# The first expert's rows of a mixture-of-experts layer picked out of SBUF by a 0/1 matrix on TensorE, with the DRAM gathers starting at the second expert and the weight requests in another order

## The reference, cut to what matters

```
h = LN1(alpha*x + m @ w_out)                    # 520 x 1024
g_prob = softmax(h @ w_group + b_group)         # one group of 4
e_logits = h @ w_router + b_router              # top 2 of the 4 experts inside it
for e in range(16):
    hid = silu(h @ w_gate[e]) * (h @ w_up[e])   # 1024 -> 512
    y += combine[:, e] * (hid @ w_down[e])      # 512 -> 1024
out = LN2(alpha*h + y)
```

## Time and profile before

| | |
|---|---|
| median of three runs | 939.65 us (938.61 to 940.93) |
| the profiled execution: its time | 937.05 us |
| its span | 935.2 us |
| mean granted TensorE clock | 0.963 |
| TensorE busy | 854.9 us, 91% of the span |
| VectorE busy | 545.4 us, 58% |
| ScalarE busy | 441.4 us, 47% |
| GpSimd busy | 173.1 us, 19% |
| DMA | 179.74 MB, 192 GB/s on average |

### The profile page before, as it was taken

How to read it: one execution, slowest core, us unless ns; L and a number is a source line. 1 busy time by engine, 2 the same in 40 slices (tenths; PEclk the granted TensorE clock), 3 DMA queues, 4 the chain that set the end, 5 groups by cost and what they waited for, 6 DMA issues and landing times.

```text
span 935.2 us, 13784 instructions
## 1 busy us (share of the span) xinstructions
PE 854.9 (91%) x5364; PEld 755.5 (81%) x5364; DVE 545.4 (58%) x613; ACT 441.4 (47%) x560; POOL 173.1 (19%) x151
## 2 busy tenths in 40 slices
PE   4999988889979899999999999489999999999990
PEld 4999976557759899999999877467888888888870
DVE  3112156665763333344222542769999999999976
ACT  4222232545553233233223211447788878778853
POOL 0085023321321000000000036141111111210103
PEclk9999999999999999999999999679999999999996
DMA  7422211810101212221221434799999999999953
GB/s 288 142 90 90 90 55 59 304 51 1 46 1 54 108 57 103 107 107 58 102 98 45 172 103 152 284 371 422 386 392 403 393 387 400 399 381 403 342 151 91
DMA packets 35835, 179.74 MB, mean 192 GB/s; under 512 B 3663, under 2 KB 11503, under 8 KB 19502
## 3 DMA queue, kind: packets, MB, share of 16 engines
q1 hardware_dynamic: 30182, 159.22, 44.1%
q0 software_dynamic: 5600, 19.99, 7.7%
q10 hardware_dynamic: 16, 0.03, 0.0%
HBM read 164.65 MB, written 16.89 MB: 194 GB/s over the span
## 4 chain that ended last, share of the span: by engine, by line
PE 84%; DVE 7%; ACT 4%; DMA 2%; issue 2%; POOL 0%; SPq 0%; DVEq 0%; ACTq 0%; POOLq 0%
PE ps L1116 8%; PE ps L1117 8%; PE ps L1118 8%; PE ps L1434 6%; PE ps L1435 6%; PE ps L1436 6%; PE ps L955 4%; PE ps L956 4%; PE ps L957 4%; PE ps L1461 3%; PE ps L1463 3%; PE ps L1462 3%; PE ps L1282 3%; ACT probs L627 2%; PE ps L1422 2%
## 5 line engine op out<-in xcount | busy, mean ns | idle before, releaser
L1920 DVE TENSOR_TENSOR elo<-eraw,ehi 128x2048 fp32r<-128x2048 f32 x96 | 218.0, 2290 | 26.2 <-ACT ehi L794 24.2
L794 ACT ACTIVATE ehi<-eraw 128x2048 fp32r<-128x2048 f32 x96 | 183.0, 1916 | 28.4 <-PE ps L1436 17.2
L1562 DVE TENSOR_TENSOR wlo<-raw,whi 128x2432 fp32r<-128x2432 f32 (+1 forms) x25 | 63.4, 2536 | 153.6 <-ACT whi L546 153.6
L1116 PE MATMUL ps<-xhi,whi 128*128 128x260 f32 x384 | 110.0, 286 | 3.5 <-DVE wlo L1736 3.5
L1117 PE MATMUL ps<-xhi,wlo 128*128 128x260 f32 x384 | 109.5, 285 | 0.0
L1118 PE MATMUL ps<-xlo,whi 128*128 128x260 f32 x384 | 109.4, 285 | 0.0
L1434 PE MATMUL ps<-ehi,xethi 128*128 128x512 f32 x256 | 103.3, 403 | 4.5 <-issue 3.2
L1435 PE MATMUL ps<-ehi,xetlo 128*128 128x512 f32 x256 | 101.2, 395 | 0.0
L1436 PE MATMUL ps<-elo,xethi 128*128 128x512 f32 x256 | 101.2, 395 | 0.0
L546 ACT ACTIVATE whi<-raw 128x2432 fp32r<-128x2432 f32 (+1 forms) x25 | 52.3, 2094 | 90.1 <-PE ps L1118 90.1
L1116 PEld LDWEIGHTS ps<-xhi,whi 128*128 128x128 f32 x384 | 73.6, 192 | 3.7 <-DVE wlo L1736 3.7
(11 more groups left out here) (365 smaller groups left out, 1887.0 us busy)
## 6 DMA issues: line engine op xcount, KB each, us to landing
eraw<-w_gate_in SPq DMA_DIRECT2D x32, 1024.0 KB, 18.1
eraw<-w_up_in SPq DMA_DIRECT2D x32, 1024.0 KB, 18.7
eraw<-w_down_in SPq DMA_DIRECT2D x32, 1024.0 KB, 20.3
raw<-wm_in SPq DMA_DIRECT2D x16, 1216.0 KB, 5.3
raw<-wz_in SPq DMA_DIRECT2D x8, 1024.0 KB, 5.3
raw<-wo_in SPq DMA_DIRECT2D x4, 1024.0 KB, 5.0
h_dram<-hall POOLq DMA_DIRECT2D x5, 416.0 KB, 3.5
f_dram<-hall POOLq DMA_DIRECT2D x5, 416.0 KB, 5.4
```

The costliest lines, as they stand in the source:

```text
L794: ac.activation(ehi[s % 3][:, :], eraw[s][:, :], ACT.Copy).then_inc(ehi_ok, 1)
L1116: pe.matmul(out, cols(whi[s], q), mh, start=k == 0, stop=False)
L1920: ve.tensor_tensor(elo[s % 3][:, :], eraw[s][:, :], ehi[s % 3][:, :].bitcast(F32), ALU.subtract)\
```

## The change

TensorE no longer waits for a gather of the first expert's rows. VectorE builds `hot0`, a 0/1 matrix of 5 x 104 tokens by 128 places for expert 0, between the two halves of the last tile's norm, and TensorE multiplies `hall` with it: 5 tiles x 8 feature groups = 40 true f32 products, whose result is the turned rows in the banks where the transposes used to put them. The slot list follows behind the picking. The weight list is made after wide product 0. Expert 1's rows are turned between the two halves of the second wide product. POOL's gathers run from expert 1 on, with the two `xe` buffers swapped. VectorE splits pieces 0 and 1 before it waits for the slot list, makes `xetlo` right after the slots, and splits piece 2 after the inputs of the weight list. SP sends pieces 3 and 8 before it waits for the rows in DRAM; pieces 4, 5, 9, 10 and on wait for the end of the picking instead of the first gather.

```diff
@@ buffers
-        gm, gd, gs = rt("gm", 2, [TR, TT]), rt("gd", 3, [TR, TT, 4]), rt("gs", 4, [TR, TT])
+        gm, gd, gs = rt("gm", 2, [TR, TT]), rt("gd", 29, [TR, TT, 4]), rt("gs", 30, [TR, TT])
+        place0, hot0 = rt("place0", 31, [TR, TT]), rt("hot0", 21, [TR, TT, CAP])
-        ltri = at("ltri", TAIL + 4096, [TR, NE, NE])
+        ltri = at("ltri", CON + 4 * C_MASK, [TR, NE, NE])
@@ SP
             sp.wait_ge(h_done, TT - 1)
             sp.wait_ge(h_last, 2)
+            expert_piece(3, 3, wu[0, 1], True)
+            expert_piece(8, 8, wd[0, 0], True)
             sp.wait_ge(h_sent, 16 * TT)
-            expert_piece(3, 3, wu[0, 1], True)
-            sp.wait_ge(xe_in[0], 16)
             sp.wait_ge(f_init, 16 * TT)
+            sp.wait_ge(xet_ps, 1)
             for n in range(2):
                 expert_piece(4 + n, 4 + n, wg[1, n], True)
-            for n in range(2):
-                expert_piece(8 + n, 8 + n, wd[0, n], True)
+            expert_piece(9, 9, wd[0, 1], True)
             expert_piece(10, 10, wg[2, 0], True)
@@ TensorE
+            pe.wait_ge(list_ok, 1)
+            pe.wait_ge(h_done, TT - 1)
+            for t in range(TT):
+                if t == TT - 1:
+                    pe.wait_ge(h_last, 2)
+                for k in range(KD):
+                    last = pe.matmul(ps[:, 4 + k // 4, (k % 4) * P:(k % 4) * P + P],
+                                     hall[:, t, :].rearrange("p (c k) -> p k c", k=KD)[:, k, :], hot0[:, t, :],
+                                     start=t == 0 and k % 4 == 0, stop=t == TT - 1, skip_group_check=True)
+            last.then_inc(xet_ps, 1)
+
             for n in range(2 * TT):
                 if n % TT == 0:
-                    pe.wait_ge(list_ok, n // TT + 1)
+                    pe.wait_ge(list_ok, n // TT + 2)
...
-            pe.wait_ge(list_ok, 3)
-            for n in range(2 * TT):
-                last = pe.matmul(ps[:, 7, P:P + NE], rowhot[...].bitcast(F32), chunkw[...], ...)
-            last.then_inc(slot_ps, 1)
+            def weight_list():
+                pe.wait_ge(list_ok, 4)
+                for n in range(2 * TT):
+                    last = pe.matmul(ps[:, 7, P:P + NE], rowhot[...].bitcast(F32), chunkw[...], ...)
+                last.then_inc(slot_ps, 1)
...
-            xet(0, 0, 16, True)
             pe.wait_ge(xet_hi, 1)
             pe.wait_ge(xet_lo, 1)
             wide(0, (0, 1), 0)
-            xet(1, 1, 16)
-            wide(2, (2, 0), 1)
+            weight_list()
+            wide(2, (2, 0), 1, between=lambda: xet(1, 0, 16))
@@ VectorE
             ve.tensor_tensor(x, x, lng[0:TR, :], ALU.mult).then_inc(h_last, 1)
+            ve.wait_ge(rank_ps, 1)
+            ve.wait_ge(rc_in, 16)
+            link(ve.scalar_tensor_tensor(place0[:, :], rank[:, :, 0], 1.0, both[:, :, 0], ALU.add, ALU.mult))
+            ve.scalar_tensor_tensor(hot0[:, :, :], row..., 1.0, place0..., ALU.add, ALU.is_equal).then_inc(list_ok, 1)
             ve.wait_ge(h_last, 1)
             ve.tensor_tensor(x, x, lnb[0:TR, :], ALU.add).then_inc(h_last, 1)
...
+            esplit(0, 0, True)
+            esplit(1, 1, True)
             ve.wait_ge(slot_ps, 1)
             found = ps[:, 6, P:P + NE]
             ve.tensor_scalar(slots[:, 0:NE], found, -1.0, float(T), ALU.min, ALU.add).then_inc(slot_ok, 1)
+            xet(0)
...
+            link(ve.tensor_copy(ltri[:, :, :], rcon...))
             ve.tensor_tensor(chunkw[:, :, :, :], picks..., wider(w12...), ALU.mult).then_inc(list_ok, 1)
-            esplit(0, 0, True)
+            esplit(2, 2, True)
             ve.wait_ge(slot_ps, 2)
             ve.tensor_copy(wslot[:, 0:NE], ps[:, 7, P:P + NE]).then_inc(wslot_ok, 1)
-            link(ve.tensor_copy(ltri[:, :, :], rcon...))
-            esplit(1, 1, True)
-            esplit(2, 2, True)
...
-            xet(0)
             esplit(3, 3)
@@ POOL
-                q = c % 2
-                if c >= 2:
-                    gp.wait_ge(xe_in[q], 16 * (c // 2))
+                q = 1 - c % 2
+                if c >= 3:
+                    gp.wait_ge(xe_in[q], 16 * ((c - 1) // 2))
                     gp.wait_ge(xet_ps, c - 1)
-                if c == 1:
+                if c == 2:
                     gp.wait_ge(xe_in[0], 16)
+                    gp.wait_ge(xet_ps, 1)
+                    gp.wait_ge(f_init, 16 * TT)
...
-            for c in range(NE):
+            for c in range(1, NE):
                 gather(c)
```

More of the change, by code:

```diff
@@ L1407, in _, with xet @@
             last.then_inc(slot_ps, 1)
-            pe.wait_ge(list_ok, 3)
-            for n in range(2 * TT):
-                last = pe.matmul(ps[:, 7, P:P + NE], rowhot[:, n // TT, n % TT, :].bitcast(F32),
-                                 chunkw[:, n // TT, n % TT, :], start=n == 0, stop=n == 2 * TT - 1)
-            last.then_inc(slot_ps, 1)
-            def xet(c, q, arrived, first=False):
+            def weight_list():
+                pe.wait_ge(list_ok, 4)
+                for n in range(2 * TT):
+                    last = pe.matmul(ps[:, 7, P:P + NE], rowhot[:, n // TT, n % TT, :].bitcast(F32),
+                                     chunkw[:, n // TT, n % TT, :], start=n == 0, stop=n == 2 * TT - 1)
+                last.then_inc(slot_ps, 1)
+            def xet(c, q, arrived):
                 pe.wait_ge(xe_in[q], arrived)
-                if not first:
-                    pe.wait_ge(xet_hi, c)
-                    pe.wait_ge(xet_lo, c)
+                pe.wait_ge(xet_hi, c)
+                pe.wait_ge(xet_lo, c)
                 for k in range(KD):
@@ L1424, in xet, with wide @@
                 last.then_inc(xet_ps, 1)
-            def wide(n, s, bank, first=False, free=None, hi=xethi, lo=xetlo):
+            def wide(n, s, bank, first=False, free=None, hi=xethi, lo=xetlo, between=None):
                 if free is not None:
@@ L1430, in wide @@
                 for j in range(2):
+                    if j and between is not None:
+                        between()
                     pe.wait_ge(elo_ok, n + j + 1)
@@ L1475, in expert @@
                 if more:
-                    xet(e + 1, 1 - odd, 16 * (i + odd) + 16)
+                    xet(e + 1, odd, 16 * i + 16)
                 down(e - 1, 6 * e + 2, (2, 0), first, between=None if more else e)
-            xet(0, 0, 16, True)
             pe.wait_ge(xet_hi, 1)
@@ L1498, in _ @@
                   .then_inc(slot_ps, 1)
-                pe.wait_ge(list_ok, 4)
+                pe.wait_ge(list_ok, 5)
                 for n in range(2 * TT):
@@ L1921, in esplit, with xet @@
                   .then_inc(elo_ok, 1)
+            def xet(c, hi=xethi, lo=xetlo):
+                ve.wait_ge(xet_hi, c + 1)
+                ve.tensor_tensor(lo[:, :, :].rearrange("p (a k) c -> p a (k c)", a=2), ps[:, 4:6, :],
+                                 hi[:, :, :].rearrange("p (a k) c -> p a (k c)", a=2).bitcast(F32), ALU.subtract)\
+                  .then_inc(xet_lo, 1)
             def over(x, n):
@@ L1955, in _ @@
             ve.tensor_tensor(x, x, lng[0:TR, :], ALU.mult).then_inc(h_last, 1)
-            ve.wait_ge(h_last, 1)
-            ve.tensor_tensor(x, x, lnb[0:TR, :], ALU.add).then_inc(h_last, 1)
             def wider(x, n):
@@ L1971, in _ @@
             ve.wait_ge(rank_ps, 1)
+            ve.wait_ge(rc_in, 16)
             rank = ps[0:TR, 7, 0:TT * NE].rearrange("p (t n) -> p t n", t=TT)
+            row = rcon[0:TR, G_ROW:G_ROW + CAP]
+            link(ve.scalar_tensor_tensor(place0[:, :], rank[:, :, 0], 1.0, both[:, :, 0], ALU.add, ALU.mult))
+            ve.scalar_tensor_tensor(hot0[:, :, :], row.rearrange("p (t n) -> p t n", t=1).broadcast_to([TR, TT, CAP]), 1.0,
+                                    place0[:, :].rearrange("p (t a) -> p t a", a=1).broadcast_to([TR, TT, CAP]),
+                                    ALU.add, ALU.is_equal).then_inc(list_ok, 1)
+            ve.wait_ge(h_last, 1)
+            ve.tensor_tensor(x, x, lnb[0:TR, :], ALU.add).then_inc(h_last, 1)
             total = ps[0:TR, 7, TT * NE:TT * NE + NE]
@@ L1977, in _ @@
             ve.tensor_tensor(chunkr[:, :, :, :], picks[:, :, :, :], wider(tokm[:, :, :], NE), ALU.mult)
-            ve.wait_ge(rc_in, 16)
-            row = rcon[0:TR, G_ROW:G_ROW + CAP]
             for c in range(2):
@@ L2000, in _ @@
             link(ve.tensor_copy(tots[:, :], total))
+            link(ve.tensor_copy(ltri[:, :, :], rcon[0:TR, G_LT:G_LT + NE * NE].rearrange("p (a e) -> p a e", a=NE)))
             ve.tensor_tensor(chunkw[:, :, :, :], picks[:, :, :, :], wider(w12[:, :, :], NE), ALU.mult).then_inc(list_ok, 1)
-            esplit(0, 0, True)
+            esplit(2, 2, True)
             ve.wait_ge(slot_ps, 2)
             ve.tensor_copy(wslot[:, 0:NE], ps[:, 7, P:P + NE]).then_inc(wslot_ok, 1)
-            link(ve.tensor_copy(ltri[:, :, :], rcon[0:TR, G_LT:G_LT + NE * NE].rearrange("p (a e) -> p a e", a=NE)))
-            esplit(1, 1, True)
-            esplit(2, 2, True)
```

5 lines of the change are left out of this document (removed).

## The result

The changed kernel takes 947.15 us in the median of four runs (946.15 to 949.05), the kernel before 939.22 in four runs beside it. The ratio on record is 1.011, 95% interval 1.0088 to 1.0131: slower by 8 to 12 us. (The quotient of these two medians is 1.0084. Beside the later runs of the kernel before, whose medians are 936.68 to 937.73, 947.15 is 9.4 to 10.5 us more, and the traces give 9.4.) The forecast was 938.65 us with a range up to 941.9, so it is wrong in sign and size. It came out as rival 3 had it, to which I gave 0.08: 949 us, the picking never brings the clock up.

What follows compares the result with a forecast made beforehand. The prediction took TensorE to bound the kernel. Six microseconds gained by the end of wide product 0, five given back (2.2 weight list, 2.8 half product), left -1.0 on the median 939.65: 938.65 us, range 936.4 to 941.9.

Steps and rivals of the forecast that it cites:

- rival 3: The picking never brings the clock up: it ends at 614.0, expert 1's turning at 632.8, +9.5, 949 us; chance 0.08.
- Step (b): TensorE's picking: 80 records, 8.9 us at full pace plus 2.25 for 4.5 us at half clock; last record starts at 607.55.
- (a): VectorE builds the 0/1 matrix between the norm's halves; TensorE's picking starts at 596.4, the last tile is complete 1.0 later.
- (c): Slot list behind the picking, 1.2 us; first wide product starts at 610.6 against 613.84, 3.2 us earlier, at full clock.
- (d): First expert's wide product 0: 24 records, 5.6 us, ends at 616.2 against 622.3; six microseconds gained.
- (e): Weight list now on TensorE's path behind wide product 0: 20 records, 2.2 us, to 618.4.
- (f): Expert 1's turning after half of wide product 1 (2.8 us): ends 622.25 against 623.30; later 2.6 us of waiting.
- The second hand-over decides: From the end of expert 1's turning to the loop a fixed 5.3 us; its shift, 1.0 us earlier, is the kernel's.
- Step (g): First gather gone; expert 1's gather starts at 609.3, lands at 619.7 to 621.0: cost 0, cover 0.2 to 1.5 us.
- Rival 1: Expert 1's gather becomes the wait: at 14 us the turning ends at 624.4, +1.1, 940.8 us; chance 0.12.
- Step (h): SP sends pieces 3 and 8 at 597.6, before the last rows are in DRAM: no effect on the path.
- Rival 2: The clock falls in the pause of (c) or of (f): +0.5 to +2.0, 940.9 us; chance 0.18.

Runs made afterwards that it cites:

- e6: Changed kernel with the picking's loaded operand read in one run of 128 floats instead of every eighth: 936.59 us, ratio 0.9994.
- e3: Changed kernel with the split of piece 4 ahead of the copy of expert 1's turned rows, on ScalarE and VectorE: 944.84 us, ratio 1.0073.
- e9: Changed kernel with e6's one-run operand, expert 0's gate and up pieces fetched in the layout to fit, and e3's order of splits: 934.87 us, ratio 0.9962.
- e11: e6 with SP's weight requests in the order of the kernel before: 937.37 us, ratio 0.999.
- e2: Changed kernel with the picking cut from five tiles to two, 32 records, leaving out rows of the first expert: 937.13 us, ratio 1.0004.
- e7: e6 with six extra unread f32 products of 512 columns ahead of the picking: 939.39 us, ratio 1.0019.
- e5: Changed kernel with `hot0` as loaded operand and `hall` streaming 512 columns, 20 records, rows then copied and turned: 941.25 us, ratio 1.0049.
- e13: e9 with six extra unread f32 products of 512 columns as one loop ahead of the rank matmuls: 935.17 us, ratio 0.9981.
- e12: Changed kernel with the picking's loaded operand read with a step of two floats instead of eight: 936.9 us, one run.
- e1: Changed kernel with seven extra unread f32 products of 512 columns in TensorE's idle time before the picking: 952.88 us, ratio 1.0137.
- e10: e9 with six extra unread f32 products of 512 columns, unrolled, five ahead of the rank matmuls and one ahead of the picking: 935.59 us, ratio 0.9977.

## Why the prediction was wrong

**Step (b) failed, in its price and in its clock.** It had "80 x 0.111 = 8.9 us" and 4.5 us at half clock. The records of rows 7 and 8 have that pace, but load an operand that lies in one run; the picking's is read with a step of eight floats, which I never compared. It measured 0.24 a record and 19.5 us, and the clock never rose in it. That is the main part of the miss: counted from T0, the second turning came 10.4 us later than foreseen, 7.8 of it up to the last record of the picking, 0.8 in the slot list behind it, and 1.9 in the first wide product, all at half clock. With the operand in one run (e6) the step is right in kind: clock up after 6.7 us, just over my upper bound of 6.1, so 8.9 + 3.35 = 12.25 us by the prediction's formula, and 12.37 measured.

**Rival 3** had the right time for half of the right reason. The clock indeed never rose in the picking. But what I set against it, that the records "have 128 columns and follow each other densely", brings the clock up in e6 and not with stepped loads, though TensorE is busy 5.00 of 5 us in both. Moved to the forecast's T0 (2.47 us earlier), the second turning ends at 635.11 - 2.47 = 632.6; the rival had 632.8. Two errors cancel in it: 80 x 0.22 let the wide product start 1.1 us too early (618.1, measured 621.63 - 2.47 = 619.16), and that product lost not 3.05 but 1.8 us to half clock (7.46 us in place of 5.63; half clock from 621.6 to about 625.7). Its turning point, 6.5 us at half clock, was about right: e6 with 6.7 us is within 0.6 us of before.

**Steps (a), (c), (d), (e), (f)** held in their order. The picking starts at T0 + 2.21 (foreseen 2.3); the weight list takes 2.30 (2.2); the third wide product waits 2.58 (2.6). Step (c) came 1 us dearer, as the list too ran at half clock: 2.28, not 1.2. Step (d) took 7.46 us, not 5.6: it counted on full clock from the start.

**"The second hand-over decides"** held: 18.04 us from the second to the third turning in both kernels, and e3 moves the third alone. Of the changed kernel's loss nothing is made up in the loop, and of e9's lead nothing is eaten.

**Step (g)**: expert 1's gather took 9.7 us and was never waited for, since all behind the picking was late. Rival 1 decides nothing in the changed kernel. **Step (h)**: without effect (e11). The late pieces landed after 16.8 to 19.3 us, well inside the slack (the earlier trace rows had 21.9 to 24.9).

**Rival 2** is real, but came in other kernels: e2 and e7 lose 1.4 to 1.5 us to it in the pause of (f), and e5, e7 and e13 another 1.5 to 1.6 in that of (c). The same pauses cost nothing in most of the other kernels, and what decides it isn't shown; the rows of the prediction left this open, and it stays so.

Still open: the transposes of rows 5 also read `xe` with a step of eight, yet take 1.04 us for eight, at full clock and with load records of 0.19 us. So a step of eight alone isn't enough to slow a load. They are one record each, and whether it is that or the transpose that spares them wasn't tried.

## What to carry to other kernels

A price taken from a row holds for the way its operands lie in SBUF, not for their shape alone: compare the step between elements of the loaded operand before using a matmul's pace, and keep it at one or two floats for true f32 products. Work that fills a pause doesn't always bring the clock up by being dense in TensorE's row: check the clock in the stretch, not the busy time. And when work is moved past a hand-over, follow it to the next one: here 5 of the 6 us that the step was to win were to be given back there, and exchanging two splits was worth more (2.4 us) than the whole picking with step one (0.6).

## What the runs showed of the hardware that was not expected

- A true f32 product of 128 columns takes 0.11 us a record at full clock with one run of floats in the loaded operand (e7), 0.12 with a step of two (e12) and 0.25 with a step of eight (e1). At half clock it is 0.21 with steps one and two, 0.24 with four and eight.
- Transposes of 128 columns that load with the same step of eight don't pay it: load records of 0.19 us (after, e5), where the picking's take 0.31 to 0.34.
- The granted clock fell from 1.00 to 0.50 some 3.3 us into a picking in which TensorE was busy without a gap (e1), and stayed at 0.50 through 19.5 us of such work (after). With a step of one it rose 5.9 to 6.7 us after the start (e6, e9, e11), with 512-column records after 6.1 (e5). In rows of 512-column products it also fell once, for some 3.3 us, with TensorE busy (e7, at 593.4).
- A pause of 1.4 to 2.6 us behind full clock was followed by a fall to half for some 3 us in some kernels (e2, e5, e7, e13) and not in others with the same pause (after, e6, e9, e10).
- A stop of 2.7 to 3.6 us without a visible releaser near the end of the three kernels with the most unrolled records on TensorE (e1, e7, e10), and half clock behind it.
